# A level of the delta-rule inversion: one chunk's products copied by ScalarE, the other's by VectorE

## The reference, cut to what matters

```
a_mat = where(strict, (k*beta) @ k.T * decay, 0) + eye(64)        # 64 x 64, unit lower triangular
sol   = triangular_solve(a_mat, [v*beta, k*beta*exp(g)])          # per head and chunk
u, w  = sol[..., :128], sol[..., 128:]
...
v_new = u - w @ s                                                 # chunk after chunk
o     = q_dec @ s + qk @ v_new
s     = s * g_end + k_end.T @ v_new
```

## Time and profile before

| | us |
|---|---|
| median of 3 runs | 2096.75 |
| the three runs | 2077.41, 2098.91, 2096.75 |
| profiled execution, own time | 2104.82 |
| profiled execution, span | 2103.0 |
| part of the span outside the four passes | 1966 |
| part of the span in the four passes (1056 to 1193) | 137 |

### The profile page before, as it was taken

How to read it: one execution, slowest core, us unless ns; L and a number is a source line. 1 busy time by engine, 2 the same in 40 slices (tenths; PEclk the granted TensorE clock), 3 DMA queues, 4 the chain that set the end, 5 groups by cost and what they waited for, 6 DMA issues and landing times.

```text
span 2103.0 us, 40763 instructions
## 1 busy us (share of the span) xinstructions
PE 1983.4 (94%) x16442; PEld 1737.9 (83%) x16442; DVE 1164.9 (55%) x1809; ACT 1030.9 (49%) x1624; POOL 156.6 (7%) x151
## 2 busy tenths in 40 slices
PE   6999999899999999999889999999989998999997
PEld 5884588787788788878778889999879998788997
DVE  4421578654643343355345667667757656667654
ACT  5333367634432233244644456555747655356653
POOL 0000100001000000100044310010020001011000
PEclk9999999889999999999999999999999999899999
DMA  8340268541233333232200056665436664325653
GB/s 270 96 125 30 70 207 249 156 121 50 80 93 97 90 91 99 83 99 82 71 4 4 24 144 187 183 186 145 132 100 188 186 179 138 101 66 145 186 174 110
DMA packets 441801, 254.55 MB, mean 121 GB/s; under 512 B 10817, under 2 KB 440513, under 8 KB 441537
## 3 DMA queue, kind: packets, MB, share of 16 engines
q1 hardware_dynamic: 441664, 252.59, 41.0%
HBM read 251.51 MB, written 1.05 MB: 120 GB/s over the span
## 4 chain that ended last, share of the span: by engine, by line
PE 84%; DVE 9%; ACT 4%; issue 2%; DMA 1%; POOL 0%; DVEq 0%; ACTq 0%; SPq 0%; POOLq 0%
PE bank L380 21%; PE bank L382 20%; PE bank L381 20%; PE bank L372 4%; PE bank L601 2%; PE bank L602 2%; DVE weights_lo L330 2%; ACT weights_hi L323 1%; PE bank L939 1%; PE bank L1170 1%; PE bank L1980 1%; PE bank L609 1%; DVE h L2604 1%; DMA ring<-ada_w 1%; PE bank L2005 1%
## 5 line engine op out<-in xcount | busy, mean ns | idle before, releaser
L330 DVE TENSOR_TENSOR weights_lo<-ring,weights_hi 128x1024 fp32r<-128x1024 f32 x472 | 578.2, 1229 | 353.5 <-ACT weights_hi L323 349.4
L323 ACT ACTIVATE weights_hi<-ring 128x1024 fp32r<-128x1024 f32 x472 | 495.7, 1054 | 383.8 <-PE bank L382 359.4
L380 PE MATMUL bank<-x_hi,weights_hi 128*128 128x256 f32 (+1 forms) x2024 | 639.0, 316 | 31.9 <-DVE x_lo L2560 11.0
L381 PE MATMUL bank<-x_lo,weights_hi 128*128 128x256 f32 (+1 forms) x2024 | 629.0, 311 | 0.0
L382 PE MATMUL bank<-x_hi,weights_lo 128*128 128x256 f32 (+1 forms) x2024 | 628.6, 311 | 0.0
L380 PEld LDWEIGHTS bank<-x_hi,weights_hi 128*128 128x128 f32 x2024 | 381.2, 188 | 67.5 <-issue 27.8
L382 PEld LDWEIGHTS bank<-x_hi,weights_lo 128*128 128x128 f32 x2024 | 381.7, 189 | 23.6
L381 PEld LDWEIGHTS bank<-x_lo,weights_hi 128*128 128x128 f32 x2024 | 381.9, 189 | 23.0 <-issue 1.4
L380 PE MATMUL bank<-hidden_hi,weights_hi 128*128 128x256 f32 (+1 forms) x864 | 270.4, 313 | 5.7 <-DVE hidden_lo L2881 3.2
L382 PE MATMUL bank<-hidden_hi,weights_lo 128*128 128x256 f32 (+1 forms) x864 | 269.9, 312 | 0.0
L381 PE MATMUL bank<-hidden_lo,weights_hi 128*128 128x256 f32 (+1 forms) x864 | 268.5, 311 | 0.0
(11 more groups left out here) (358 smaller groups left out, 2338.3 us busy)
## 6 DMA issues: line engine op xcount, KB each, us to landing
ring<-mlp_w SPq DMA_DIRECT2D x128, 512.0 KB, 3.9
ring<-ada_w SPq DMA_DIRECT2D x96, 512.0 KB, 4.6
ring<-w_ffn_in SPq DMA_DIRECT2D x88, 512.0 KB, 4.0
ring<-w_ffn_out SPq DMA_DIRECT2D x32, 512.0 KB, 3.6
ring<-gdn_w_in SPq DMA_DIRECT2D x24, 512.0 KB, 3.9
ring<-even_w_in SPq DMA_DIRECT2D x18, 512.0 KB, 4.1
ring<-w_out SPq DMA_DIRECT2D x16, 512.0 KB, 3.7
ring<-w_in_a SPq DMA_DIRECT2D x14, 512.0 KB, 3.8
```

What stands on the lines that cost most here:

```text
L323: nc.scalar.activation(w_hi[:, g % AHEAD, :], ring[:, g % RAW, :], ACT.Copy).then_inc(hi_done[g % AHEAD].sem, 1)
L330: nc.vector.tensor_tensor(w_lo[:, g % AHEAD, :], ring[:, g % RAW, :], w_hi[:, g % AHEAD, :].bitcast(F32), ALU.subtract).then_inc(lo_done[g ...
L380: pe.matmul(dst, lhs[0](k), rhs[0](k), start=start and k == 0, stop=False)
L381: pe.matmul(dst, lhs[0](k), rhs[1](k), start=False, stop=False)
```

## The change

In every level and for every z, ScalarE copies only chunk 0's bank and signals `qx`. VectorE copies chunk 1's bank in a new function, `dve_gdn_turned`, which waits for `xr` and signals a new semaphore `qy`. TensorE's z step waits for both. In VectorE's queue the new function stands just ahead of whatever came ahead of the level: before `vn` at levels 1 and 2, but behind `ss` and the decays of the level before, and behind `below` (or `query`) at level 4. It copies z = 0 and then z = 1, ahead of the level's predicated copies of z = 0.

```diff
         def pe_gdn_z(pe, p, lv):
             for z, u in units(p):
                 pe.wait_ge(N["qx"], nth(LEVELS, p, lv, z))
+                pe.wait_ge(N["qy"], nth(LEVELS, p, lv, z))
...
         def act_gdn_level(act, p, lv):
             for z, u in units(p):
                 act.wait_ge(N["xr"], nth(LEVELS, p, lv, z))
-                for c in range(2):
-                    ins = nc.scalar.activation(QX[:, z, c].rearrange("p m n -> p (m n)"), bank_of(p, z, c)[:, :], ACT.Copy)
-                ins.then_inc(N["qx"], 1)
+                nc.scalar.activation(QX[:, z, 0].rearrange("p m n -> p (m n)"), bank_of(p, z, 0)[:, :], ACT.Copy)\
+                    .then_inc(N["qx"], 1)
...
+        def dve_gdn_turned(dve, p, lv):
+            for z, u in units(p):
+                dve.wait_ge(N["xr"], nth(LEVELS, p, lv, z))
+                nc.vector.tensor_copy(QX[:, z, 1].rearrange("p m n -> p (m n)"), bank_of(p, z, 1)[:, :]).then_inc(N["qy"], 1)
+
...
             for p in range(4):
+                dve_gdn_turned(dve, p, 0)
                 dve_gdn_level(dve, p, 0)
                 for st in range(2):
+                    dve_gdn_turned(dve, p, 1 + st)
                     if p >= 1:
                         dve_gdn_vn(dve, p - 1, st)
                     dve_gdn_level(dve, p, 1 + st)
                     if p >= 1:
                         dve_gdn_ss(dve, p - 1, st)
                     if p < 3 and st == 0:
                         dve_gdn_decays(dve, p + 1)
+                dve_gdn_turned(dve, p, 3)
                 dve_gdn_level(dve, p, 3)
                 if p < 3:
                     dve_gdn_below(dve, p + 1)
                 else:
                     dve_gdn_query(dve, 2)
+                dve_gdn_turned(dve, p, 4)
                 dve_gdn_level(dve, p, 4)
```

More of the change, by code:

```diff
@@ L1884, in dve_odd_in @@
             normed(VB - 1)
-        gdn_names = ("gl", "g", "d", "size", "e", "bb", "eb", "kk", "aa", "eye", "first", "xr", "qx", "zz", "xt", "xb", "xw",
+        gdn_names = ("gl", "g", "d", "size", "e", "bb", "eb", "kk", "aa", "eye", "first", "xr", "qx", "qy", "zz", "xt", "xb", "xw",
                      "u", "uc", "wt", "wtc", "kend", "ws", "vn", "su", "ss", "sg", "clear", "qk", "eu", "qkt", "g2", "qe", "qd",
```

## The result

| | before | change |
|---|---|---|
| median, us (22 runs each, side by side) | 2099.26 | 2106.47 |
| lowest and highest, us | 2077.41, 2106.86 | 2099.79, 2117.2 |
| ratio to before, 95% interval | | 1.005 [1.0031, 1.0069] |
| profiled execution, own time, us | 2104.82 | 2113.21 |

The change makes the kernel slower by about 0.5%. The forecast was 2096.4 with a range up to 2105; the median lies 1.5 us above its upper end. Of the three signs of being wrong that I had set, two came: the stage differs by over 4 us, and the clock drops within it. What was built is what the text said: the page, which answers to the earlier trace rows, has 40 more VectorE instructions and 40 fewer of ScalarE.

What follows compares the result with a forecast made beforehand. TensorE, busy 94% of the span, was taken to bound the kernel, with about 6 us of copy waits as ceiling. Terms -1.2 - 0.8 + 0.15 + 1.45 = -0.4 us gave 2096.4 us against the 2096.75 median, range 2077 to 2105.

Steps and rivals of the forecast that it cites:

- three signs of being wrong: `vn` released by a copy, the four-pass stage differing by over 4 us, or the clock dropping within it.
- pass 1: Pass 1: copies fit ahead of `vn`, level 1 and level 4 z 1 start 0.41 earlier; -0.8 us in all.
- rival B: Pass 3, level 4: longer TensorE idling lets the clock fall, costing 10.8 us, so 2107 us; chance 4%.
- the queue at (3,4): Pass 3, level 4: VectorE's copies queue behind `query`, delaying z products, predicated copies and values; +1.45 us.
- the extra wait: TensorE's z steps: 40 more waits, mostly long met; taken as 0, bounds 0 to 2 us.
- the gains of passes 0 and 1: Quicker copies let z products start earlier where little covers them: -1.2 us in pass 0, -0.8 in pass 1.
- the pauses: TensorE's stops without a releaser before L1995 and L1980: kept unchanged, bounds -4.1 to +4.1 us.
- pass 2, level 4: Pass 2, level 4: z 0's copy queues behind `below`, its products 0.8 us later; +0.15 us taken.
- the copies: 40 VectorE copies replace 40 of ScalarE's 80: 686 ns each, 27 us in all, bounds 440 ns to 1.37 us.
- `vn`: Pass 1: z 1's copy ends 0.36 us ahead of `vn`, which the `ws` products still release.
- rival A: ScalarE and VectorE reading PSUM at once slow VectorE's copies to 1.37 us: +6.0, 2102.8 us; chance 8%.
- Rival D: Whole run: the median falls to the level of one faster earlier run, 2077 us; chance 15%.

Runs made afterwards that it cites:

- split_query: Changed kernel with `query` of pass 2 split, four of its eight instructions ahead of pass 3, level 4 and four behind; ratio 1.0021 [0.9999, 1.0044].
- short_copies: Kernel before with ScalarE's copies cut from 512 to 32 columns everywhere but pass 0, level 0; ratio 0.9977 [0.9949, 1.0004].
- filled: Changed kernel with TensorE computing the q products of z 1 in pass 3, level 4 three times over; ratio 1.0022 [0.9994, 1.0051].
- filled_third: Third profile of the changed kernel with q products of z 1 in pass 3, level 4 computed three times; single run of 2093.41 us.
- change_again: The changed kernel run again, unedited, for a second profile; ratio to the kernel before 1.0039 [1.0015, 1.0062].

## Why the prediction was wrong, step by step

**The sum against the profiles.** Change minus before, means of three profiles each: pass 0 -0.05 (predicted -1.2), pass 1 +0.96 (-0.8), pass 2 +0.05 (+0.15), pass 3 up to level 4 +0.24 (0), (3,4) +3.56 (+1.45). Together +4.8 where I had -0.4.

**Failed: rival B's refusal.** I wrote "Against it: it stood at 1.00 in the whole stage through all its gaps", and gave 4%. The stage of before has no gap like the one that I had just predicted; that its smaller gaps, 1.3 at most of those without a releaser, left the clock alone said little about 1.4 to 1.6 us at the end of a level full of short waits. The clock fell in three profiles of three. The price was off as well, the other way: I took 10.8 us from a stretch of 25 us; the stretch is 3.4 or 6.8 us long and costs about 2. Nor does the gap alone decide: split_query's clock fell there without it. Likelier and cheaper, it belonged in the sum.

**Mis-sized: the queue at (3,4).** "All of 1.45 arrives there" had the right mechanism: the z products start 1.56 later relative to q (3.30 to 4.86), behind `query` as described, and where the clock was still full the values start 1.54 later. The 0.09 that is missing in 1.45 is the hop. I wrote of the extra wait that "its hop merely replaces the hop of the other one", and took 0.05 for both. But wherever TensorE waited for a copy, its z products start 0.05 us behind the end of ScalarE's (12 or 13 places in each profile of before) and 0.15 behind VectorE's (8 places in each of the change). The +3.56 is 1.54 of queue and 2.0 of clock.

**Failed: the gains of passes 0 and 1.** The chain was right, its hop too short: the copies of level 0 of pass 0 start and end as computed, and the products of z 1 0.1 later than that. Its timeline, to be held against the earlier trace rows (q of z 1, copies, predicated copies, z products):

```profile
1056.02 0.69 PE L1980 MATMUL bank<-arena 64*64 64x64 f32 x32
...
1057.15 0.69 DVE L2245 COPY arena<-bank 128x512 f32<-128x512 f32 x1 [0.45 <-PE bank L1985]
1057.80 0.78 DVE L2253 COPY_PREDICATED arena<-tables,bank 128x256 f32<-128x256 int32 x2
...
1057.99 0.69 PE L1996 MATMUL bank<-arena 64*64 64x64 f32 x32 [0.26 <-DVE arena L2245]
```

From q of z 1 to its z products it is 1.97 instead of 2.26, so 0.29 is saved where I had 0.41; the hop of 0.15 takes the rest. Counted from that q, level 3 starts 0.60 earlier (11.93 against 12.53), where I had 0.8; in the means of three profiles it is 0.33 (12.25 against 12.58). Then come the key products:

```profile
1069.98 0.33 PE L1960 MATMUL bank<-arena 64*64 64x64 f32 x4
1070.69 1.09 PE L1960 MATMUL bank<-arena 64*64 64x64 f32 x59 [0.38 <-issue]
```

Before, these 64 ran through in 1.19 us; here they take from 1069.98 to 1071.84, 1.86, with a stop in them that no releaser ends, and the z products behind them start just 0.03 ahead of before. What failed is "I keep them as they are". I had even bounded the pauses, at -4.1 to +4.1, and then let the gains stand whole. Counted at the matmuls, the pauses of pass 0 make 1.25, 0.71 and 0.98 us in the three profiles of before, and 1.03, 1.55 and 1.55 in those of the change. Without them the pass is 0.4 shorter, not 1.2; the rest of the missing gain is the smaller step and what I can't resolve. Other kernels say the same: the ten profiles with the changed copies in pass 0 took 28.18 to 30.03 us there, six with the old ones 28.03 to 28.95. short_copies points the same way: the passes hardly answer to the copies at all. The profile has the supplier too. The DMA view of before, for 1056 to 1195 (packets, MB, share of 16 engines):

```profile
q8 instruction: 34, 0.56, 1.7%
```

34 packets of 16 KB in 139 us, one every 4.1 us. The count of TensorE's instructions fits 250 or so to a packet, so I take these to be its program; that each pause is a late packet was argued from the times (pauses end about 1.1 us before the next packet starts), not shown by an experiment of its own. The Trainium skill (Runtime: NRT & Kernel Launch, section Instruction fetch mechanics) says that crossing a 16 KiB block is mostly hidden. For this stream of 64x64 products the traces disagree, if these are the crossings: pauses of 0.3 to 1.3 us, and 2.9 us of shorter waits in short_copies that went into longer pauses.

**Mis-sized: pass 1.** -0.8 predicted, +0.96 found. Level 1, where I had booked 0.41 of gain, took 8.27 in all three profiles instead of 7.90 in the mean. Its z products of z 1 do start 0.30 sooner behind q (1.97 against 2.27), but the `su` products behind them take longer, 2.37, 2.09 and 2.09 us against 1.64. Before, and then the change:

```profile
1094.25 1.64 PE L2065 MATMUL bank<-a,arena 64*64 64x128 f32 x32
```

```profile
1091.91 2.37 PE L2066 MATMUL bank<-a,arena 64*64 64x128 f32 x32
```

Why they do is not shown. +0.68 of the pass lies in level 4 (9.64 to 10.32), behind `below`, and there a pause again, in `first`:

```profile
1114.47 0.51 PE L1969 MATMUL bank<-tables,arena 64*64 64x64 f32 x11 [1.04 <-issue]
```

It is less sure than the table makes it look: five other profiles with the same code in pass 1 took 34.10 to 34.83 us, six profiles without the change in pass 1 33.57 to 34.36.

**Held: pass 2, level 4.** 9.14 to 9.39 us, +0.25 against +0.15 predicted. The copies queue behind `below` as read from the earlier trace rows:

```profile
1144.47 1.40 DVE L2232 TENSOR_TENSOR spare<-bank,spare 128x256 f32<-128x256 f32 x4
...
1145.79 1.27 DVE L2245 COPY arena<-bank 128x512 f32<-128x512 f32 x2
...
1146.62 1.29 PE L1996 MATMUL bank<-arena 64*64 64x64 f32 x64 [0.90 <-DVE arena L2245]
```

**Held: the copies, `vn`, the extra wait.** VectorE's copy takes 689 ns (686 predicted), and ScalarE's next to it 598 (600 before). In 36 of the 40 places the two overlap, at 690 and 598 ns in the mean, and in the other four they took 681 and 597. So reading PSUM at the same time costs neither engine more than 1%: rival A is out. `vn` of pass 1, level 2 still starts when `ws` releases it, 0.34 us behind the end of the copy, where I had 0.36:

```profile
1098.27 0.69 DVE L2245 COPY arena<-bank 128x512 f32<-128x512 f32 x1 [0.33 <-PE bank L1985]
...
1099.30 2.01 DVE L2283 TENSOR_TENSOR a<-a,bank 64x512 f32<-64x512 f32 x3 [0.33 <-PE bank L2054]
```

The extra wait, where it was long met, costs nothing that the stage shows. Rival D, another level of the run, did not matter: over 22 runs the one at 2077.41 stayed the exception.

**Open.** Of the 8.7 us between the means, the four passes explain 4.8. The rest lies outside them, in code that did not change. The granted clock has a trace of it: over all runs its mean is 0.97498 with the change and 0.97775 before, which is 12.1 us more at half speed, or 6.0 us lost, and the stretches in (3,4) make 2.8 of these. By this count some 3 us are lost to the clock elsewhere. Where, I could not show, as single executions of one kernel differ too much: outside the four passes the three profiles of before took 1950.5 to 1964.6 us with 75 to 96 us at half clock, those of the change 1950.5 to 1969.3 with 85 to 109.

## What to carry to other kernels

Moving work to an idle engine moves it into that engine's queue: look for the one place where a long instruction stands ahead of it, because one level of twenty made 3.6 of the 4.8 us lost in the passes here, and leave that place with the old engine. A gap that you predict in a TensorE that was dense is also a question to the clock, and must be priced, even if smaller gaps did nothing. And where the profile shows TensorE pausing with no releaser in a stream of tiny matmuls, don't book a few tenths saved per step: the pauses may take them back.

## What the runs showed of the hardware

- A wait of TensorE of 1.36 to 1.72 us, in a stage where it is busy for 90%, went with a stretch of 3.4 or 6.8 us at 1.2 GHz, in 3 of 3 profiles of the change and 2 of 2 of the same place alone; the stretch began between 0.6 us ahead of the wait's end and 2.0 behind it. Each of these waits had a pause of 0.71 to 1.07 us shortly before. In filled, pauses of 0.80 to 1.07 and 0.74 us, apart from each other, were not followed by one in 3 of 3 profiles. In split_query a pause of 1.07 behind a wait of 0.41 was, while the same pair was not in filled_third, nor at that place in change_again. In filled's pass 0 a pause of 1.20 was.
- Such a stretch cost 1.5 to 2.8 us in these five profiles, beyond the 1.54 of the wait: in the first profile z products of 64 took 1.99 instead of about 1.3 us and the values 5.59 instead of 3.60.
- TensorE's z products start 0.05 us behind the end of a ScalarE copy that they waited for and 0.15 behind that of a VectorE copy, in all 37 and 24 such places of the three profiles of before and of the change.
- ScalarE and VectorE copying two different PSUM banks at once took 598 and 690 ns for 128x512 float32; where they did not overlap, 597 and 681.
- Forty semaphore waits long met added no time that the stage shows (136.81 us against 137.70).
- Copies cut from 600 to 196 ns removed 3.4 us of TensorE's wait for ScalarE and gave back 0.7: waits with no releaser grew in their place, to 6.8 us from 3.4 to 4.6.
